# The experts' head: the first expert's rows picked from x by one-hot products on TensorE, and the second expert's rows turned inside the first gate product

## The chip, the cores and the metric

The kernel runs on one core of a Trainium2 chip. The metric is the device time of one launch in microseconds (us). An idle engine or a faster instruction counts only where the end of the launch moves. The five engines named here are TensorE (PE in the profile), VectorE (DVE), ScalarE (ACT), GpSimd (POOL) and SyncE (SP, which here only issues DMAs).

## What is computed

Two layers of a first kind are followed by two layers of a second kind, on 512 tokens of width 1024. The change touches only the mixture of experts at the end of each layer of the first kind, so it acts twice per launch:

```python
def _hier_moe(x, wg, bg, we, be, w_gate, w_up, w_down):
    ...
    ep, ei = lax.top_k(jax.nn.softmax(elog, -1), TOP_K)
    ep = ep / jnp.sum(ep, -1, keepdims=True)
    eid = gi * EXPERTS_PER_GROUP + ei
    combine = jnp.sum(jax.nn.one_hot(eid, N_EXPERTS, dtype=F32) * (gp * ep)[..., None], axis=2)
    h = jax.nn.silu(jnp.einsum('bsd,edf->bsef', x, w_gate)) * jnp.einsum('bsd,edf->bsef', x, w_up)
    h = h * combine[..., None].astype(h.dtype)
    return jnp.einsum('bsef,efd->bsd', h, w_down)
```

Each token uses 2 of 16 experts. The kernel gathers the up to 128 tokens of an expert into 128 slots, computes the expert for these rows alone, and scatters the results back.

## The kernel before

Every engine runs its own list of instructions in the order in which the code writes them; between engines only semaphores order the work. Nothing is planned by a scheduler, so an instruction written behind a waiting one waits too.

`expert_stage` (lines 2449 to 2740) treats 16 experts, e = 0 to 15, in a fixed order. The router ahead of it leaves `rank` (for each token and expert the slot number, or none) and `facts` (token number, row number, weight). For each expert, the steps are:

- **place(e)** (DVE, L2632) compares the slot numbers with the ranks. It gives `take`, a one-hot matrix of 4 tiles of 128 tokens by 128 slots. Two buffers alternate.
- **find_facts(e)** (PE, L2519): 4 products of `take` with the facts. **keep_facts(e)** (DVE, L2637 to L2639) turns them into `to_token`, `to_row` and `weight`, and signals `index_ready`. place(e+2) and, on PE, find_facts(e+1) wait for these.
- **gather(e)** (POOL, L2711), an indirect DMA, fetches the expert's rows of x from memory into `xg`, which has three buffers. `xg` is cleared first (L2722), because empty slots are not fetched.
- **turn_x(e)** (PE, L2530): 8 transposes of `xg` into two PSUM banks. **x_pair(e)** (ACT, L2588) copies each bank as the rounded part `xt_hi`, and **x_rest(e)** (DVE, L2645) computes the remainder `xt_lo`.
- **gate_up_product(e)** (PE, L240 to L242): 24 matmuls, 12 for each half of the 1024 rows of weights, into one bank.
- ACT applies silu (L2609), DVE multiplies (L2678, `hidden`), PE transposes the result (**turn_hidden**, L2550), ACT and DVE split it (L2615, L2686), and PE multiplies it with the down weights (12 matmuls). The result is scattered (L2718).

Weights arrive in units of 1 MB through a ring of six raw buffers (L2397). Each unit is split by ACT into its rounded part (`split_hi`, L2404) and by DVE, or POOL for the down weights, into the remainder (`split_lo`, L2408). SP loads unit u only when unit u-6 is split. The gate and up weights of expert 0 are units 0 and 1, those of expert 1 units 2 and 3.

The head is what stands ahead of the loop over the experts. On DVE: place(0), place(1), then keep_facts(e) and place(e+2) for e = 0 to 3, then split_lo of units 0 and 1, then x_rest(0) and x_rest(1). On PE: find_facts(0) to (3), turn_x(0), turn_x(1). On ACT: split_hi of units 0 and 1, x_pair(0), x_pair(1). In the loop's first round ACT splits units 2 and 3 and then applies silu, and DVE splits units 2 and 3 and then computes hidden(0). A whole second pass over the experts would run where an expert has more than 128 tokens; the profiled execution has one pass per layer.

Of the kernel before, what the change touches and what calls it, by code (L numbers as in the profile page):

```python
# [1773 lines left out]
def out_ffn_stage(env, stage, first, first_ffn, yt, xo, x, gains, small, out, saved):  # L1774
# [44 lines left out]
    with ExitStack() as local:  # L1819
# [133 lines left out]
        with nc.Block() as block:  # L1953
# [237 lines left out]
            def _(dve):  # L2191
# [148 lines left out]
                for m in range(len(downs)):  # L2340
# [13 lines left out]
                 "hidden_turned", "hidden_hi", "hidden_lo", "down_done", "stored_first", "stored_second", "rows_sent", "rows_seen")  # L2354
# [94 lines left out]
def expert_stage(env, gate_up, down, rank, facts, next_units, small, x, lower_rows, entry_loads):  # L2449
# [15 lines left out]
     hidden_lo, down_done, stored_first, stored_second, rows_sent, rows_seen) = (env.sem("experts", n) for n in EXPERT_EVENTS)  # L2465
# [9 lines left out]
    with ExitStack() as local:  # L2475
# [10 lines left out]
        og = tile("out", 2, D)  # L2486

# [3 lines left out]
        with nc.Block() as block:  # L2491
# [21 lines left out]
            def _(pe):  # L2513
# [8 lines left out]

                def turn_x(e):
                    pe.wait_ge(gathered[e % 3], 16 * (e // 3 + 1))
                    for b in range(2):
                        if e:
                            pe.wait_ge(x_lo, 2 * (e - 1) + b + 1)
                        for j in range(4):
                            k = 4 * b + j
                            last = nc.tensor.transpose(x_bank(b)[:, j, :], xg[:, e % 3, k * P:(k + 1) * P], ident)  # L2530
                        last.then_inc(x_turned, 1)

                def gate_up_product(e):
# [3 lines left out]
                    for half in range(2):  # L2537
# [5 lines left out]
                        last.then_inc(w.used, 1)  # L2543

# [25 lines left out]
                turn_x(0)  # L2570
                turn_x(1)
# [12 lines left out]
            def _(act):  # L2584
# [13 lines left out]
                for e in range(2):  # L2598
                    x_pair(e)
                for e in range(E):  # L2600
                    if e + 1 < E:
                        for half in range(2):
                            w.split_hi(act, w.at["gu", e + 1] + half)
                    if e == E - 1:
                        w.split_hi(act, w.at["down", e])
# [19 lines left out]
            def _(dve):  # L2625
# [32 lines left out]

                place(0)
# [6 lines left out]
                for e in range(2):  # L2666
                    x_rest(e)
                for e in range(E):
                    if e + 1 < E:
                        for half in range(2):  # L2670
                            w.split_lo(v, w.at["gu", e + 1] + half)
                    if e == E - 1:
                        w.split_lo(v, w.at["down", e])
# [32 lines left out]
            def _(pool):  # L2706
# [15 lines left out]
                nc.gpsimd.memset(xg[:, :, :], 0.0).then_inc(padded, 1)  # L2722
                pool.wait_ge(padded, 1)
                for e in range(3):
                    gather(e)
                for e in range(E):
# [8 lines left out]
                for s in range(3):  # L2735
                    pool.wait_ge(gathered[s], 16 * len(range(s, E, 3)))
# [842 lines left out]
```

## Time and profile before

| | us |
|---|---|
| median of 3 runs | 2600.57 |
| lowest and highest | 2599.93, 2602.46 |
| the profiled execution, whole | 2597.38 |
| its span, first to last instruction | 2595.6 |

PE is busy for 92% of the span, DVE 68%, ACT 51%, POOL 24%. The times in the rows below are counted from the span's start. A row of the timeline begins with the start and the duration of a group of equal instructions; "x8" is their count; the brackets at its end hold how long the engine stood idle ahead of the group and who ended that.
### The profile page before, as it was taken

To read this page: it belongs to the slowest core of one execution; us is meant where nothing else is said; L and a number is where in the kernel's file an instruction comes from. 1 tells how busy PE (TensorE), PEld (TensorE's weight loads), DVE (VectorE), ACT (ScalarE), POOL (GpSimd) and SP (SyncE) were. 2 spreads that over 40 slices of the span, in tenths; PEclk is the share of its full clock that TensorE was granted. 3 is DMA by queue.
4 is the path that set the end of the run, shared out by engine and by line. 5 is a ranking of instruction groups with operands and counts; after the bars stand their busy time and mean duration, and the time that the engine had idled before them with its cause. 6 is when DMAs were issued, how large, how long until landed. Compare 5 with 4: busy or idle time off the path is not lost. (4 is left out here: it accounts for less than half of the span.)

```text
span 2595.6 us, 37232 instructions
## 1 busy us (share of the span) xinstructions
PE 2391.2 (92%) x14216; PEld 2015.2 (78%) x14216; DVE 1752.6 (68%) x2747; ACT 1318.1 (51%) x2638; POOL 614.4 (24%) x337
## 2 busy tenths in 40 slices
PE   7999896997999896996998899999999989999999
PEld 7866675776866775775786789998887857899987
DVE  1755757874655756876698669995256985699942
ACT  3446625773546615775655744444157456444421
POOL 2401304771401303782360110000023501100000
PEclk9999987998999987998998999999999999999999
DMA  4210027983210017993120023323222201123221
GB/s 161 81 39 1 1 99 288 353 331 125 83 49 1 1 58 285 349 335 135 66 98 17 5 91 118 111 82 106 85 91 73 91 1 48 72 102 116 100 87 72
DMA packets 54994, 285.84 MB, mean 110 GB/s; under 512 B 13216, under 2 KB 13216, under 8 KB 28704
## 3 DMA queue, kind: packets, MB, share of 16 engines
q1 hardware_dynamic: 45600, 266.65, 28.1%
q0 software_dynamic: 9216, 16.80, 1.7%
q8 instruction: 114, 1.87, 0.3%
q14 instruction: 64, 0.52, 0.1%
HBM read 275.02 MB, written 25.17 MB: 116 GB/s over the span
## 5 line engine op out<-in xcount | busy, mean ns | idle before, releaser
L229 POOL TENSOR_TENSOR weights_lo<-weights_raw,weights_hi 128x2048 fp32r<-128x2048 f32 (+4 forms) x53 | 239.2, 4515 | 729.7 <-issue 358.6
L240 PE MATMUL ps<-x_operands,weights_hi 128*128 128x256 f32 x1232 | 347.7, 282 | 5.8 <-DVE weights_lo L1945 5.1
L241 PE MATMUL ps<-x_operands,weights_hi 128*128 128x256 f32 x1232 | 348.8, 283 | 0.0
L242 PE MATMUL ps<-x_operands,weights_lo 128*128 128x256 f32 x1232 | 348.2, 283 | 0.0
L215 ACT ACTIVATE weights_hi<-weights_raw 128x2048 fp32r<-128x2048 f32 (+5 forms) x86 | 148.2, 1723 | 307.9 <-PE ps L242 288.4
L240 PEld LDWEIGHTS ps<-x_operands,weights_hi 128*128 128x128 f32 x1232 | 233.7, 190 | 8.4 <-DVE weights_lo L1945 6.8
L242 PEld LDWEIGHTS ps<-x_operands,weights_lo 128*128 128x128 f32 x1232 | 231.7, 188 | 0.0
L241 PEld LDWEIGHTS ps<-x_operands,weights_hi 128*128 128x128 f32 x1232 | 231.0, 187 | 0.0
L240 PE MATMUL ps<-weights_hi,attn_ht_hi 128*128 128x512 f32 (+2 forms) x576 | 204.7, 355 | 4.3 <-DVE weights_lo L229 2.3
L241 PE MATMUL ps<-weights_lo,attn_ht_hi 128*128 128x512 f32 (+2 forms) x576 | 201.2, 349 | 0.0
L242 PE MATMUL ps<-weights_hi,attn_ht_lo 128*128 128x512 f32 (+2 forms) x576 | 200.5, 348 | 0.0
L229 DVE TENSOR_TENSOR weights_lo<-weights_raw,weights_hi 128x2048 fp32r<-128x2048 f32 (+3 forms) x33 | 65.1, 1973 | 179.6 <-ACT weights_hi L215 179.6
L240 PE MATMUL ps<-weights_hi,x_operands 128*128 128x512 f32 x384 | 152.9, 398 | 6.2 <-PEq L263 6.2
L241 PE MATMUL ps<-weights_lo,x_operands 128*128 128x512 f32 x384 | 152.9, 398 | 0.0
L240 PE MATMUL ps<-weights_hi,xt_hi 128*128 128x480 f32 (+2 forms) x384 | 138.9, 362 | 5.8 <-DVE weights_lo L229 2.5
L1939 ACT ACTIVATE weights_hi<-ffn_w_sums 128x1024 fp32r<-128x1024 f32 x66 | 70.0, 1060 | 133.4 <-DVE ffn_w_sums L2249 133.4
L242 PE MATMUL ps<-weights_hi,xt_lo 128*128 128x480 f32 (+2 forms) x384 | 136.1, 354 | 0.0
L241 PE MATMUL ps<-weights_lo,xt_hi 128*128 128x480 f32 (+2 forms) x384 | 135.8, 354 | 0.0
L240 PEld LDWEIGHTS ps<-weights_hi,attn_ht_hi 128*128 128x128 f32 x576 | 110.1, 191 | 28.0 <-issue 9.1
L242 PE MATMUL ps<-weights_hi,ffn_hidden_lo 128*128 128x512 f32 x320 | 125.8, 393 | 0.0
L242 PEld LDWEIGHTS ps<-weights_hi,attn_ht_lo 128*128 128x128 f32 x576 | 109.9, 191 | 13.4
L241 PEld LDWEIGHTS ps<-weights_lo,attn_ht_hi 128*128 128x128 f32 x576 | 110.2, 191 | 11.7
(531 smaller groups left out, 6259.5 us busy)
## 6 DMA issues: line engine op xcount, KB each, us to landing
weights_raw<-in_stream SPq DMA_DIRECT2D x96, 1024.0 KB, 4.7
weights_raw<-in_expert_gu SPq DMA_DIRECT2D x34, 1024.0 KB, 9.5
expert_raw<-in_expert_gu SPq DMA_DIRECT2D x30, 1024.0 KB, 9.7
expert_raw<-in_expert_down SPq DMA_DIRECT2D x18, 1024.0 KB, 8.5
weights_raw<-in_expert_down SPq DMA_DIRECT2D x14, 1024.0 KB, 8.2
weights_raw<-in_stream SPq DMA_DIRECT2D x12, 960.0 KB, 4.5
ffn_raw<-in_stream SPq DMA_DIRECT2D x10, 1024.0 KB, 4.8
weights_raw<-in_stream SPq DMA_DIRECT2D x8, 700.0 KB, 9.5
```

The costliest lines, as they stand in the source:

```text
L215: self.nc.scalar.activation(self.split_tiles(u)[0][:, 0:n], self.env.raw[:, u % self.RAW, 0:n], ACT.Copy).then_inc(self.hi_ready, 1)
L229: eng.tensor_tensor(lo[:, 0:n], self.env.raw[:, u % self.RAW, 0:n], hi[:, 0:n].bitcast(F32), ALU.subtract).then_inc(self.lo_ready, 1)
L240: nc.tensor.matmul(out, a[0], b[0], start=start, stop=False, **more)
L241: nc.tensor.matmul(out, a[0], b[1], start=False, stop=False, **more)
L242: return nc.tensor.matmul(out, a[1], b[0], start=False, stop=stop, **more)
L1939: nc.scalar.activation(ring(g)[0], quarter(c, w_of[p]), ACT.Copy).then_inc(w_hi_done, 1)
```

## The change

Expert 0's rows are no longer gathered. DVE writes its one-hot matrix a second time, in float32, into the space of `hidden` (`first_take`), ahead of place(0). PE multiplies x, which lies in SBUF, with it (`pick_x`): for each of 8 chunks of 128 columns 4 products, one for each tile of tokens. This gives the transposed rows directly in the bank where turn_x(0) put them. The picks are written between the find_facts of the head, two chunks behind each. turn_x(1) moves from the head into the middle of gate_up_product(0); x_pair(1) on ACT and x_rest(1) on DVE move between the splits of units 2 and 3. POOL clears each buffer of `xg` by itself and gathers experts 1 and 2 in between; gather(3) no longer waits behind a gather(0).

```diff
@@ expert_stage
+        first_take = hidden[:, :, :].rearrange("p a c -> p (a c)").rearrange("p (t s) -> p t s", t=T)
...
+                def pick_x(chunks):
+                    pe.wait_ge(first_placed, 1)
+                    for k in chunks:
+                        for t in range(T):
+                            last = nc.tensor.matmul(x_bank(k // 4)[:, k % 4, :], x[:, t, k * P:(k + 1) * P],
+                                                    first_take[:, t, :], start=(t == 0), stop=(t == T - 1))
+                    if k % 4 == 3:
+                        last.then_inc(x_turned, 1)
+
...
                         last.then_inc(w.used, 1)
+                        if e == 0 and half == 0:
+                            turn_x(1)
...
                 for e in range(AHEAD):
                     find_facts(e)
-                turn_x(0)
-                turn_x(1)
+                    pick_x(range(2 * e, 2 * e + 2))
...
                 for half in range(2):
                     w.split_hi(act, half)
-                for e in range(2):
-                    x_pair(e)
+                x_pair(0)
...
                             w.split_hi(act, w.at["gu", e + 1] + half)
+                            if e == 0 and half == 0:
+                                x_pair(1)
...
+                v.tensor_tensor(first_take, env.slot_numbers.unsqueeze(1).to_broadcast([P, T, SLOTS]),
+                                per_tile(rank[:, :, EXPERT_ORDER[0]], SLOTS), ALU.is_equal).then_inc(first_placed, 1)
                 place(0)
                 place(1)
...
-                for e in range(2):
-                    x_rest(e)
+                x_rest(0)
...
                             w.split_lo(v, w.at["gu", e + 1] + half)
+                            if e == 0 and half == 0:
+                                x_rest(1)
...
-                nc.gpsimd.memset(xg[:, :, :], 0.0).then_inc(padded, 1)
-                pool.wait_ge(padded, 1)
-                for e in range(3):
+                for e in (1, 2):
+                    nc.gpsimd.memset(xg[:, e, :], 0.0).then_inc(padded, 1)
+                    pool.wait_ge(padded, e)
                     gather(e)
+                nc.gpsimd.memset(xg[:, 0, :], 0.0).then_inc(padded, 1)
+                pool.wait_ge(padded, 3)
```

PE's list at the head of the expert stage, before (L2519 are the facts, L2530 the turned rows of experts 0 and 1, `weights_hi` the first gate product):

```order
L2519 MATMUL ps<-slot_facts,expert_take 128x4 x16
L2530 MATMUL ps<-consts,expert_xg 128x128 x16
L240 MATMUL ps<-weights_hi,expert_xt_hi 128x512
L241 MATMUL ps<-weights_lo,expert_xt_hi 128x512
L242 MATMUL ps<-weights_hi,expert_xt_lo 128x512
```

The same place after (L2521 are the facts, L2529 the picks):

```order
L2521 MATMUL ps<-slot_facts,expert_take 128x4 x4
L2529 MATMUL ps<-expert_hidden,x 128x128 x8
L2521 MATMUL ps<-slot_facts,expert_take 128x4 x4
L2529 MATMUL ps<-expert_hidden,x 128x128 x8
L2521 MATMUL ps<-slot_facts,expert_take 128x4 x4
L2529 MATMUL ps<-expert_hidden,x 128x128 x8
L2521 MATMUL ps<-slot_facts,expert_take 128x4 x4
L2529 MATMUL ps<-expert_hidden,x 128x128 x8
```

The facts of experts 1, 2 and 3 now stand behind 8, 16 and 24 picks, and the 8 transposes of expert 1 behind the first 12 matmuls of the gate product.

ACT's list there, before (L2404 is split_hi, L2588 x_pair, L2609 silu):

```order
L2404 ACTIVATE weights_hi<-weights_raw 128x2048 x2
L2588 ACTIVATE expert_xt_hi<-ps 128x512 x4
L2404 ACTIVATE expert_w_hi<-weights_raw 128x2048
L2404 ACTIVATE expert_w_hi<-expert_raw 128x2048
L2609 ACT_TABLE_LOAD
L2609 ACTIVATE expert_gate<-ps 128x256
```

And after (L2405 is split_hi, L2600 x_pair, L2622 silu):

```order
L2405 ACTIVATE weights_hi<-weights_raw 128x2048 x2
L2600 ACTIVATE expert_xt_hi<-ps 128x512 x2
L2405 ACTIVATE expert_w_hi<-weights_raw 128x2048
L2600 ACTIVATE expert_xt_hi<-ps 128x512 x2
L2405 ACTIVATE expert_w_hi<-expert_raw 128x2048
L2622 ACT_TABLE_LOAD
L2622 ACTIVATE expert_gate<-ps 128x256
```

The split of unit 3 now stands behind the copies of expert 1's turned rows; on DVE the remainders move in the same way.

## Rows read from the trace of the kernel before

**Rows 1.** Timeline of PE, layer 1's head: start, us, line, count, [idle before].
```profile
401.50 1.01 PE L2519 MATMUL ps<-slot_facts,expert_take 128*128 128x4 f32 x4 [4.70 <-DVE expert_take L2632]
...
413.52 1.97 PE L2530 MATMUL ps<-consts,expert_xg 128*128 128x128 f32 x8 [6.63 <-DMA expert_xg<-x_rows,expert_token]
417.29 1.97 PE L2530 MATMUL ps<-consts,expert_xg 128*128 128x128 f32 x8 [1.80 <-DMA expert_xg<-x_rows,expert_token]
418.91 0.78 PE L240 MATMUL ps<-weights_hi,expert_xt_hi 128*128 128x512 f32 x1
...
420.34 0.63 PE L240 MATMUL ps<-weights_hi,expert_xt_hi 128*128 128x512 f32 x1
420.77 0.50 PE L241 MATMUL ps<-weights_lo,expert_xt_hi 128*128 128x512 f32 x1
...
421.33 0.40 PE L240 MATMUL ps<-weights_hi,expert_xt_hi 128*128 128x512 f32 x1
...
424.15 0.39 PE L240 MATMUL ps<-weights_hi,expert_xt_hi 128*128 128x512 f32 x1
```
**Rows 2.** Window in the loop: us, busy PE, PEld, DVE, ACT, POOL, PEclk, DMA, GB/s.
```profile
442.00:462.00 20.00, 19.39 (x98) 15.81 (x97) 17.06 (x23) 15.13 (x16) 14.95 (x7) 1.00 0.94 348
```
**Rows 3.** Timeline of PE, the hidden transposes of experts 0 and 1.
```profile
426.70 0.44 PE L2550 MATMUL ps<-consts,expert_hidden 128*128 128x128 f32 x2 [0.99 <-DVE expert_hidden L2678]
...
438.06 0.44 PE L2550 MATMUL ps<-consts,expert_hidden 128*128 128x128 f32 x2 [1.28 <-DVE expert_hidden L2678]
```
**Rows 4.** Timeline of DVE, layer 1's head and first two rounds.
```profile
400.75 1.29 DVE L2632 TENSOR_TENSOR expert_take<-consts,expert_rank 128x512 fp32r<-128x512 f32 x2 [2.78 <-PEq L120]
...
406.93 0.16 DVE L2637 TENSOR_SCALAR expert_token<-ps 128x1 int32<-128x1 f32 x1 [0.57 <-PE ps L2519]
...
407.13 0.68 DVE L2632 TENSOR_TENSOR expert_take<-consts,expert_rank 128x512 fp32r<-128x512 f32 x1
...
423.94 2.28 DVE L2408 TENSOR_TENSOR expert_w_lo<-expert_raw,expert_w_hi 128x2048 fp32r<-128x2048 f32 x1
426.17 0.48 DVE L2678 SCALAR_TENSOR_TENSOR expert_hidden<-expert_gate,expert_weight,ps 128x256 f32<-128x256 f32 x1
428.24 0.42 DVE L2686 TENSOR_TENSOR expert_ht_lo<-ps,expert_ht_hi 128x256 fp32r<-128x256 f32 x1 [1.59 <-ACT expert_ht_hi L2615]
...
430.13 3.08 DVE L2632 TENSOR_TENSOR expert_take<-consts,expert_rank 128x512 fp32r<-128x512 f32 x1
...
437.54 0.47 DVE L2678 SCALAR_TENSOR_TENSOR expert_hidden<-expert_gate,expert_weight,ps 128x256 f32<-128x256 f32 x1
```
**Rows 5.** Groups of PE by line and shape: count, busy, mean ns, idle before.
```profile
L3280 PE MATMUL ps<-proj,attn_prob_t 128*128 128x128 f32 x160 | 26.7, 305 | 0.0
```
**Rows 6.** Timeline of PE elsewhere: float32 work at the half and the full clock.
```profile
237.06 3.46 PE L1200 MATMUL ps<-consts,cols 128*128 128x128 f32 x16 [3.07 <-PEq L1331]
...
1402.67 1.49 PE L3280 MATMUL ps<-proj,attn_prob_t 128*128 128x128 f32 x6
1404.09 0.92 PE L3251 MATMUL ps<-qk_t 64*128 64x384 f32 x4
...
1439.87 1.06 PE L3280 MATMUL ps<-proj,attn_prob_t 128*128 128x128 f32 x8
```
**Rows 7.** Windows over stretches in which the clock rose or didn't, columns as in rows 2.
```profile
400.00:417.00 17.00, 5.94 (x24) 5.28 (x24) 10.82 (x22) 6.30 (x5) 7.14 (x5) 0.50 0.91 362
...
240.30:243.70 3.40, 3.40 (x10) 1.58 (x10) 1.83 (x3) 3.40 (x11) 0.91 (x2) 1.00 0.00 0
1398.50:1404.00 5.50, 5.50 (x23) 4.49 (x23) 5.12 (x15) 3.21 (x13) 0.00 (x0) 0.50 0.00 1
```
**Rows 8.** Timeline of ACT, layer 1's first round.
```profile
421.59 1.91 ACT L2404 ACTIVATE expert_w_hi<-expert_raw 128x2048 fp32r<-128x2048 f32 x1
423.52 1.28 ACT L2609 ACT_TABLE_LOAD   x1
```
**Rows 9.** Timeline of POOL, layer 1's head.
```profile
400.71 2.66 POOL L2722 MEMSET expert_xg<- 128x3072 f32 x1 [84.41 <-issue]
```

More of the change, by code:

```diff
@@ L2353 @@
 EXPERT_EVENTS = ("padded", "placed", "facts_ready", "index_ready", "x_turned", "x_hi", "x_lo", "silu_done", "hidden_done",
-                 "hidden_turned", "hidden_hi", "hidden_lo", "down_done", "stored_first", "stored_second", "rows_sent", "rows_seen")
+                 "hidden_turned", "hidden_hi", "hidden_lo", "down_done", "stored_first", "stored_second", "rows_sent", "rows_seen",
+                 "first_placed")
 class ExpertWeights:
@@ L2464, in expert_stage @@
     (padded, placed, facts_ready, index_ready, x_turned, x_hi, x_lo, silu_done, hidden_done, hidden_turned, hidden_hi,
-     hidden_lo, down_done, stored_first, stored_second, rows_sent, rows_seen) = (env.sem("experts", n) for n in EXPERT_EVENTS)
+     hidden_lo, down_done, stored_first, stored_second, rows_sent, rows_seen, first_placed) = (env.sem("experts", n) for n in EXPERT_EVENTS)
     gathered = [env.sem("experts", f"gathered{s}") for s in range(3)]
@@ L2521, in find_facts @@
                     last.then_inc(facts_ready, 1)
+                def pick_x(chunks):
[6 more added lines that the diff above has]
+                        last.then_inc(x_turned, 1)
                 def turn_x(e):
-                    pe.wait_ge(gathered[e % 3], 16 * (e // 3 + 1))
+                    pe.wait_ge(gathered[e % 3], 16 * len(range(e % 3 or 3, e + 1, 3)))
                     for b in range(2):
@@ L2735, in _ @@
                 for s in range(3):
-                    pool.wait_ge(gathered[s], 16 * len(range(s, E, 3)))
+                    pool.wait_ge(gathered[s], 16 * len(range(s or 3, E, 3)))
                 for s in range(2):
```

## The prediction, made before the changed kernel ran

> **What bounds the kernel now.** I read the timeline of each engine over the head of layer 1's expert stage first, then the windows for TensorE's clock. Layer 2 runs the same code with the same counts, so what layer 1 gives counts twice. The stage begins at 400.7, and PE then stands idle: 6.63 us until expert 0's gathered rows land at 413.5, and 1.80 us more for expert 1's [rows 1]. The first gate product starts at S = 418.91, behind the transposes of expert 1. In the loop behind the head PE is busy 19.39 of 20 us [rows 2], so what the head loses or gains at the start of that dense part stays. Between the two lies one more place to look at: turn_hidden(0) at 426.70 and turn_hidden(1) at 438.06 both wait for DVE, 0.99 and 1.28 us [rows 3]. From the second of them on PE runs without a wait of size. So 438.06 is the point at which I settle the account: how much later or earlier does turn_hidden(1) come?
>
> Three engines must deliver for S: PE the turned rows, ACT the rounded copies, and DVE the remainders. DVE was free early: its last facts began at 406.93, the last place at 407.13, the two weight splits followed, and then it waited for the turned rows [rows 1, 4].
>
> **Removed: the waits for two gathers.** They are worth 6.63 and 1.80 us on PE [rows 1], if nothing else takes their place. The rest of this part asks what does.
>
> **Added: the picks, and what they hold up.** first_take is one more compare on DVE: two of them take 1.29 us together, 0.68 alone [rows 4], so each costs 0.6. find_facts(0) moves from 401.50 [rows 1] to 402.1. A pick is a float32 product. In the trace each such product of the code is two instructions: L3280 of this shape, 80 products in the code's list over both layers, stands there 160 times [rows 5]. So 32 picks are 64 instructions. Six of L3280 at the half clock take 1404.09 - 1402.67 = 1.42 us, 0.237 each; eight at the full clock take about 0.12 each [rows 6]. The clock is 0.50 over the whole head [rows 7]. Sixteen transposes of the same size, begun at the half clock, take 3.46, about 0.21 each [rows 6]; that is the lower bound, and I take 0.235. The 4 fact products of an expert cost 0.96 at the half clock [rows 1]. For DVE what counts is when the facts of expert 3 are out: behind 4 groups of facts and 3 groups of 16 pick instructions. At the half clock that is 4 x 0.96 + 48 x 0.235 = 15.1 us.
>
> The picks keep PE busy, so the clock should rise under them. Before, the steps of the matmuls fall from 0.43 (420.34 to 420.77) to 0.235 (12 from 421.33 to 424.15), so it rose at about 421.1, 3.8 us after the unbroken work that began at 417.29 [rows 1]. It rose within 3.2 us after the transposes that began at 237.06; yet it stayed at the half for the 5.5 us of unbroken work from 1398.5 [rows 1, 6, 7]. I take 4.8 us, so 406.9, with 3.1 and 5.6 as ends. The other 10.3 us of half-clock work then take 0.51 of that, and the facts of expert 3 are out at 406.9 + 5.3 = 412.2, where before it was 406.9.
>
> The Trainium skill (TensorE: Matmul & The Clock Gate, Part 1) says that the point at which the clock rises is run-variable for the same kernel. These rows differ likewise, 3.1 us to over 5.5. By one fixed ramp of 3.8 us, facts would be out at 411.7, and the sum would be lower by about 1 us a layer.
>
> DVE cannot go on without these facts, because keep_facts(3) and place(5) stand ahead of its weight splits. From the end of the facts it needs 0.04 to begin, 0.20 to the place, 0.6 for it, 2 x 2.23 for two splits back to back, the distance from one's start to the next instruction at 423.94, and 1.29 for the two halves of x_rest(0), the same size as two places [rows 4]: together 6.6. So x_lo is complete at 418.75, and with 0.05 for the signal S = 418.8. ACT is no hindrance: the picks end at 412.2 + 16 x 0.12 = 414.1, and its two copies are done before DVE wants them at 417.5. **The gather's wait is thus replaced by a wait for DVE, and the gain of S is 0.1 us.** With the ends of the ramp, S is 417.9 to 419.2.
>
> **Moved: turn_x(1) into the gate product.** Before, its 8 transposes lay ahead of S. Now PE does 12 matmuls, 8 transposes, 12 matmuls. What follows hangs on T, the time at which the transposes are done: x_pair(1), then split_hi of unit 3 on ACT, split_lo of unit 3 on DVE, and only then hidden(0). From T, ACT's split of unit 3 begins 0.55 later and takes 1.9 [rows 8]; DVE's split follows at once and hidden(0) starts 2.23 after the split's start, as 423.94 to 426.17 [rows 4]. With the signals that is T + 4.73, and turn_hidden(0) is 0.53 later [rows 3, 4], T + 5.26. The silu path is shorter: the second 12 matmuls end at T + 2.8 and ACT's table load of 1.28 at T + 3.7 [rows 8].
>
> From hidden(0) to hidden(1) it was 11.37 us, of which DVE waited 1.59 for ACT [rows 4], which now has less of a backlog when hidden(0) comes; I count 0.6 of it as regained. hidden(1) comes at T + 4.73 + 10.77 = T + 15.5, and turn_hidden(1) at T + 16.0. PE's own path, two products and a down product, would be ready for it at T + 15.2.
>
> **T itself.** At the full clock T = S + 12 x 0.235 + 8 x 0.11 + 0.15 = S + 3.85 [rows 1]. But PE stands idle from 414.1 to 418.8, 4.7 us. In this trace the idle 3 us ahead of 237.06 were enough for 0.50 [rows 6, 7]. So the product starts at the half clock, as before; only that before, the 8 transposes had already used up 1.6 us of the ramp. The half-clock price of 12 matmuls and 8 transposes is 12 x 0.43 + 8 x 0.22 + 0.15 = 7.07; with a ramp of 4.8 again, T = S + 4.8 + 2.27 x 0.53 + 0.15 = S + 6.15 = 424.95.
>
> turn_hidden(1) = 440.95, against 438.06 [rows 3]: **2.9 us later in layer 1**, and as much in layer 2. Sum: +5.8 us. The rest of the stage shifts along: SP loads units 6 and 7 about 5 us later, since their buffers are split later, but the loop asks for them only at its third expert. gather(1) is written behind facts that come at 408, and PE asks for it at 424, in the middle of the product; before, it landed at 417.2 even behind a gather(0) [rows 1]. gather(2) and gather(3) have more room still.
>
> **A port rule.** POOL now clears `xg` in three pieces, and two of them lie beside DVE's later places. Before, the clearing from 400.71 to 403.37 lay over two places at 0.6 each, as fast as alone [rows 4, 9]; the place at 430.13, beside a POOL tensor operation, took 3.08. I cost the clearing at nothing. The Trainium skill (GPSIMD Engine Reference, 1. Specifications) has GpSimd's SBUF interfaces shared with VectorE, with contention for instructions of two SBUF inputs. These rows agree for the tensor operation and not for the clearing.
>
> **The rivals.**
> 1. The clock is already full, or rises at once, under the picks: facts of expert 3 at 402.1 + 7.7 = 409.8, S = 416.4, then the product at full clock, T = 420.3, turn_hidden(1) at 436.3: -1.8 a layer, -3.6 in all, 2597.0. It decides from T under 422. For it: the picks are unbroken work. Against: 0.50 for the 17 us from 400 [rows 7]. A chance of 0.04; over 0.2% faster would need still more, such as DVE getting its facts without waiting for picks.
> 2. The clock holds through PE's idle 4.7 us: T = S + 3.85, turn_hidden(1) at 438.65, +0.6 a layer: 2601.8. Chance 0.16.
> 3. The downstream chain takes up more than 0.6 us, or the ramp is short both times: +1 to +2 a layer, 2603 to 2604.5. Chance 0.2.
> 4. The clearing or the gathers' issue slow DVE's place(4) and place(5), one of them to 3.08 as beside the tensor operation: +2.4 a layer more than the forecast, 2611.2. Chance 0.06.
> 5. The picks do not raise the clock: facts at 417.2, S = 423.8, T = S + 6.15: +8 a layer, 2616. Against: 16 such transposes from 237.06 raised it by 240.3 [rows 6, 7]. Chance 0.05.
>
> **How the numbers follow.** The forecast, with 0.49, is +5.8 us: profiled 2597.4 + 5.8 = 2603.2, and since that execution lay 3.2 us under the median, 2600.6 + 5.8 = 2606.4. Its own range, from the two ends of each ramp, is +4 to +8. The range of 8 in 10 takes in rival 3, most of 2 and rival 4: 2601.5 to 2611.5. Within 0.2%, 5.2 us, is about what a measurement of this kernel can tell from no change. Slower by more: two thirds of the forecast (0.33), rivals 4 and 5, some tails (0.06): 0.50. Faster: 0.03. Same: 0.47.
>
> **What would show it.** In the changed profile: 64 pick instructions, the first at about 403; the clock rising between 405 and 408; PE's last facts near 412; DVE's two splits from 413 to 417.5; S near 418.8, waiting for DVE's remainder and not for a DMA; the half clock over most of the first 12 matmuls; turn_hidden(1) near 441. The prediction is wrong if DVE begins its splits before 411, if the clock is 1.00 at S, or if turn_hidden(2) follows turn_hidden(1) by less than the 10.35 us of PE's round, which would mean slack that I do not see.

## The result and the profile after

The changed kernel takes **2608.67 us** (median of 12 runs, 2602.49 to 2611.92); the kernel before, in 12 runs beside it, 2600.25 (2597.91 to 2603.96). The ratio is 1.0031, with a 95% interval of 1.0024 to 1.0039: slower by 8.4 us, 0.3%. The forecast was 2606.4, range 2601.5 to 2611.5. Of the runs reported below, one of experiment 5 (3996 us) and two of the kernel before (3990 and 6726 us) are left out of the ratios; without them no median below moves by more than 0.3 us.

| profiled execution | before | after |
|---|---|---|
| whole time, us | 2597.38 | 2609.35 |
| span, us | 2595.6 | 2607.6 |
| PE busy, us | 2391.2 | 2412.0 |
| mean granted clock | 0.959 | 0.957 |

The profiled pair differs by 12.0 us where the medians differ by 8.4. Of the 12.0, the two heads hold 7.9; 0.4 lie ahead of the first head, 1.8 between the heads and 1.9 behind the second, in steps of about 1 us, in stages in which the two kernels are the same. At one such step the clock differs: it is 0.50 in 740.5 to 743.5 us after, and 1.00 in the same place before, 734.2 to 737.2.

The account of a head runs as the prediction set it up, from its first DVE instruction to turn_hidden(1):

| from the head's first DVE instruction, us | before, layer 1 | after, layer 1 | before, layer 2 | after, layer 2 |
|---|---|---|---|---|
| first gate product (S) | 18.16 | 18.44 | 17.76 | 18.40 |
| turn_hidden(0) | 25.95 | 29.14 | 25.76 | 29.09 |
| turn_hidden(1) | 37.31 | 42.47 | 37.14 | 39.92 |
| against before | | +5.16 | | +2.78 |

So the gathers' wait is gone, and S is still 0.3 and 0.6 us later than before. From turn_hidden(1) of layer 1 the distance stays: turn_hidden(2) follows 10.37 us later before and 10.35 after.

First PE's timeline in layer 1, the answer to [rows 1] and [rows 3] (start, us, engine, line, operation, count, [idle before]). L2521 are the facts, L2529 the picks, L240 the gate product, L2541 the turned rows, L2563 the hidden transposes.

```profile
402.47 1.02 PE L2521 MATMUL ps<-slot_facts,expert_take 128*128 128x4 f32 x4 [5.30 <-DVE expert_take L2645]
403.35 3.76 PE L2529 MATMUL ps<-expert_hidden,x 128*128 128x128 f32 x16
406.76 0.99 PE L2521 MATMUL ps<-slot_facts,expert_take 128*128 128x4 f32 x4
...
410.61 2.03 PE L2529 MATMUL ps<-expert_hidden,x 128*128 128x128 f32 x16
412.40 0.59 PE L2521 MATMUL ps<-slot_facts,expert_take 128*128 128x4 f32 x4
412.84 2.03 PE L2529 MATMUL ps<-expert_hidden,x 128*128 128x128 f32 x16
...
419.56 0.79 PE L240 MATMUL ps<-weights_hi,expert_xt_hi 128*128 128x512 f32 x1 [4.69 <-DVE expert_xt_lo L2658]
...
423.96 1.04 PE L2541 MATMUL ps<-consts,expert_xg 128*128 128x128 f32 x8
...
430.26 0.69 PE L2563 MATMUL ps<-consts,expert_hidden 128*128 128x128 f32 x2 [2.46 <-DVE expert_hidden L2694]
430.74 1.91 PE L2541 MATMUL ps<-consts,expert_xg 128*128 128x128 f32 x8
...
443.59 0.41 PE L2563 MATMUL ps<-consts,expert_hidden 128*128 128x128 f32 x2 [0.30 <-PE ps L242]
```

The 6.63 us for a DMA ahead of the turned rows [rows 1] are now 4.69 for DVE's remainder, ahead of S. The wait ahead of turn_hidden(0) has grown from 0.99 to 2.46, and the wait of 1.28 ahead of turn_hidden(1) [rows 3] is gone, because PE itself is late there. In layer 2 the same two places read:

```profile
1024.21 0.44 PE L2563 MATMUL ps<-consts,expert_hidden 128*128 128x128 f32 x2 [2.45 <-DVE expert_hidden L2694]
...
1035.04 0.44 PE L2563 MATMUL ps<-consts,expert_hidden 128*128 128x128 f32 x2 [0.76 <-DVE expert_hidden L2694]
```

The picks, in the view of one line (the shortest, median and longest duration of one in ns; 64 instructions in each layer):

```profile
L2529 PE MATMUL ps<-expert_hidden,x x128: 274/275/561, 403.3 to 1008.6; 128*128 128x128 f32 x128
```

Spacing is what counts, not this latency: group to group, 16 picks took 406.76 - 403.35 = 3.41 us at the half clock, 0.213 each, and 412.40 - 410.61 = 1.79 at the full clock, 0.112 each.

DVE's timeline, the answer to [rows 4]:

```profile
413.02 0.16 DVE L2650 TENSOR_SCALAR expert_token<-ps 128x1 int32<-128x1 f32 x1 [1.34 <-PE ps L2521]
...
413.23 0.68 DVE L2645 TENSOR_TENSOR expert_take<-consts,expert_rank 128x512 fp32r<-128x512 f32 x1
413.82 4.49 DVE L2409 TENSOR_TENSOR weights_lo<-weights_raw,weights_hi 128x2048 fp32r<-128x2048 f32 x2
...
418.23 1.28 DVE L2658 TENSOR_TENSOR expert_xt_lo<-ps,expert_xt_hi 128x512 fp32r<-128x512 f32 x2
...
425.22 1.29 DVE L2658 TENSOR_TENSOR expert_xt_lo<-ps,expert_xt_hi 128x512 fp32r<-128x512 f32 x2 [3.51 <-ACT expert_xt_hi L2600]
...
427.52 2.29 DVE L2409 TENSOR_TENSOR expert_w_lo<-expert_raw,expert_w_hi 128x2048 fp32r<-128x2048 f32 x1 [1.01 <-ACT expert_w_hi L2405]
...
429.73 0.47 DVE L2694 SCALAR_TENSOR_TENSOR expert_hidden<-expert_gate,expert_weight,ps 128x256 f32<-128x256 f32 x1
```

The two splits stand behind facts that PE delivers only between its picks; behind the splits stands x_rest(0), which S needs. Below it, the chain that the move of turn_x(1) made: copies, split on ACT, split on DVE, hidden(0).

The windows for the clock, the answer to [rows 7] and [rows 2] (us; busy PE, PEld, DVE, ACT, POOL with counts; then PE's granted clock, DMA share, GB/s). The last is layer 2.

```profile
402.50:409.20 6.70, 6.70 (x31) 6.70 (x32) 2.30 (x9) 2.18 (x2) 0.16 (x1) 0.50 0.97 401
408.60:414.50 5.90, 5.90 (x53) 5.90 (x52) 2.45 (x10) 2.40 (x2) 4.15 (x4) 0.95 1.01 425
419.60:422.50 2.90, 2.90 (x7) 2.32 (x8) 2.11 (x1) 0.00 (x0) 0.00 (x0) 0.50 0.97 357
423.00:427.50 4.50, 4.50 (x25) 3.65 (x23) 1.29 (x2) 2.89 (x3) 0.00 (x0) 1.00 0.96 395
430.30:436.00 5.70, 5.70 (x21) 5.12 (x22) 3.80 (x7) 4.06 (x5) 4.79 (x2) 0.50 0.54 187
442.00:462.00 20.00, 19.39 (x98) 15.77 (x97) 16.96 (x23) 14.94 (x17) 15.53 (x6) 1.00 0.84 300
1024.30:1031.00 6.70, 6.70 (x37) 5.78 (x38) 5.68 (x8) 5.63 (x6) 5.84 (x2) 1.00 0.57 175
```

The fifth row is the difference between the layers. Behind the idle 2.46 us PE worked at the half clock for about 6 us in layer 1 (430.30 to 436.00), and in layer 2, behind an idle 2.45, it did not (1024.30 to 1031.00). The slow stretch of PE also holds up ACT and, through it, DVE's chain to hidden(1):

```profile
437.83 1.92 ACT L2405 ACTIVATE expert_w_hi<-weights_raw 128x2048 fp32r<-128x2048 f32 x1 [2.75 <-PE ps L242]
...
439.78 2.29 DVE L2409 TENSOR_TENSOR expert_w_lo<-weights_raw,expert_w_hi 128x2048 fp32r<-128x2048 f32 x1 [1.40 <-ACT expert_w_hi L2405]
```

POOL's timeline, the answer to [rows 9]:

```profile
409.04 1.21 POOL L2727 DMA_INDIRECT expert_xg<-x_rows,expert_token  x1 [7.00 <-DVE expert_weight L2652]
410.26 0.97 POOL L2739 MEMSET expert_xg<- 128x1024 f32 x1
...
413.03 0.97 POOL L2742 MEMSET expert_xg<- 128x1024 f32 x1
```

The clearing from 413.03 lies over DVE's place from 413.23, which took 0.68, as long as alone.

### The profile page after: what moved, and what is told of

Same layout as the page of the kernel before. It is cut to its first block and busy times, and to the rows that moved or that the text cites. A ratio compares the mean times of both kernels' runs of the same rounds, so it can differ in the third digit from the quotient of the medians.

```text
span 2607.6 us, 37460 instructions
## 1 busy us (share of the span) xinstructions
PE 2412.0 (93%) x14328; PEld 2030.2 (78%) x14328; DVE 1751.2 (67%) x2749; ACT 1320.0 (51%) x2638; POOL 611.5 (23%) x339
## 5 line engine op out<-in xcount | busy, mean ns | idle before, releaser
L240 PE MATMUL ps<-x_operands,weights_hi 128*128 128x256 f32 x1232 | 349.3, 284 | 5.7 <-DVE weights_lo L1945 5.1
L240 PEld LDWEIGHTS ps<-x_operands,weights_hi 128*128 128x128 f32 x1232 | 231.3, 188 | 8.4 <-DVE weights_lo L1945 6.8
L240 PE MATMUL ps<-weights_hi,attn_ht_hi 128*128 128x512 f32 (+2 forms) x576 | 203.8, 354 | 5.0 <-DVE weights_lo L229 2.3
L240 PE MATMUL ps<-weights_hi,x_operands 128*128 128x512 f32 x384 | 152.9, 398 | 6.7 <-PEq L263 6.6
L240 PE MATMUL ps<-weights_hi,xt_hi 128*128 128x480 f32 (+2 forms) x384 | 138.1, 360 | 6.1 <-DVE weights_lo L229 2.5
L240 PEld LDWEIGHTS ps<-weights_hi,attn_ht_hi 128*128 128x128 f32 x576 | 109.4, 190 | 28.9 <-issue 9.1
L242 PEld LDWEIGHTS ps<-weights_hi,attn_ht_lo 128*128 128x128 f32 x576 | 109.6, 190 | 13.3
```

The costliest lines, as they stand in the source:

```text
L240: nc.tensor.matmul(out, a[0], b[0], start=start, stop=False, **more)
L242: return nc.tensor.matmul(out, a[1], b[0], start=False, stop=stop, **more)
```

## Experiments

All are edits of the changed kernel and compute the whole output; each was timed in 11 runs, beside runs of the kernel before on the same chip: 33 for experiments 1 to 4, 33 for 5 to 8, 27 for 9 to 11. "After" is the changed kernel. A ratio is that to the kernel before, with its 95% interval; times given as differences are of medians. The last two columns of the table at the end of this section compare each head sum with the time.

**1. DVE's splits ahead of the last facts.** The theory: S waits for DVE, and DVE for facts behind picks.

```diff
                 for e in range(AHEAD):
+                    if e >= 2:
+                        w.split_lo(v, e - 2)
                     keep_facts(e)
                     place(e + 2)
-                for half in range(2):
-                    w.split_lo(v, half)
                 x_rest(0)
```

> The changed kernel with one edit on DVE: the split of unit 0 stands ahead of keep_facts(2) and that of unit 1 ahead of keep_facts(3), instead of both behind keep_facts(3). Theory (DVE, held up by facts that stand behind the picks, sets the start S of the first gate product): S comes about 2.9 us sooner in each layer (416.6 on the scale of the changed profile, where it was 419.56), PE's idle gap ahead of S shrinks from 4.7 to under 2 us, the launch is 6 to 9 us faster than the changed kernel, about 2600 to 2602. Rival (the first product would then wait for something else, or the loss lies in the moved transposes alone): under 2 us gained against the changed kernel, 2607 or more.

Measured: 2599.69 against 2599.28, ratio 1.0002 (0.9993 to 1.0011). S comes 14.90 and 14.81 us behind the head's start, 3.5 sooner than after, and the launch is 8 to 9 us faster than after, as the theory had it. PE's timeline, layer 1:

```profile
416.04 0.50 PE L240 MATMUL ps<-weights_hi,expert_xt_hi 128*128 128x512 f32 x1 [1.79 <-DVE expert_xt_lo L2658]
...
419.93 1.09 PE L2541 MATMUL ps<-consts,expert_xg 128*128 128x128 f32 x8 [0.81 <-DMA expert_xg<-x_rows,expert_token]
...
426.28 0.44 PE L2563 MATMUL ps<-consts,expert_hidden 128*128 128x128 f32 x2 [2.45 <-DVE expert_hidden L2694]
```

DVE's, with the splits now in the stretches in which it waited for facts:

```profile
408.01 0.68 DVE L2645 TENSOR_TENSOR expert_take<-consts,expert_rank 128x512 fp32r<-128x512 f32 x1
408.69 2.29 DVE L2409 TENSOR_TENSOR weights_lo<-weights_raw,weights_hi 128x2048 fp32r<-128x2048 f32 x1
411.10 0.68 DVE L2645 TENSOR_TENSOR expert_take<-consts,expert_rank 128x512 fp32r<-128x512 f32 x1
411.70 2.29 DVE L2409 TENSOR_TENSOR weights_lo<-weights_raw,weights_hi 128x2048 fp32r<-128x2048 f32 x1
414.10 0.68 DVE L2645 TENSOR_TENSOR expert_take<-consts,expert_rank 128x512 fp32r<-128x512 f32 x1
```

Mending DVE's order alone takes back the whole loss of the change. It pays twice: S is sooner, and the gap ahead of it is 1.79 instead of 4.69, and the product starts at the full clock (the first matmul takes 0.50 us, where it took 0.79 in the changed kernel). The 2.45 ahead of turn_hidden(0) is still there. A new wait of 0.81 for gather(1) stands ahead of the transposes. On POOL the issue of that gather now takes 3.02 us instead of 1.21, beside DVE's first split:

```profile
409.05 3.02 POOL L2727 DMA_INDIRECT expert_xg<-x_rows,expert_token  x1 [7.00 <-DVE expert_weight L2652]
```

**2. turn_x(1), with its copies and remainders, back ahead of the gate product.** The theory: the move made hidden(0) late. PE's part of the edit; x_pair(1) on ACT and x_rest(1) on DVE go back behind x_pair(0) and x_rest(0) likewise.

```diff
                         last.then_inc(w.used, 1)
-                        if e == 0 and half == 0:
-                            turn_x(1)
...
                     pick_x(range(2 * e, 2 * e + 2))
+                turn_x(1)
```

> The changed kernel with the second half of the change undone: expert 1's rows are turned ahead of the first gate product again, and copied and split right behind those of expert 0. Theory (turning them inside the product delays hidden(0), since unit 3 is split behind them): S comes later, 420 to 421, since PE waits for gather(1), but hidden(0) comes about 2 us sooner (427.8 instead of 429.73), the launch is 3 to 5 us faster than the changed kernel, 2603 to 2606. Rival (the wait for gather(1) only takes the place of the delay): within 1.5 us of the changed kernel.

Measured: 2602.79, 1.0010 (1.0001 to 1.0019). S is 0.4 and 0.8 later than after, hidden(0) 2.5 and 1.8 sooner, turn_hidden(1) 37.67 and 38.62 behind the head's start. So the moved step costs more inside the product than it would ahead of it. One stated reason, that PE would wait for gather(1), fell:

```profile
418.27 1.94 PE L2541 MATMUL ps<-consts,expert_xg 128*128 128x128 f32 x8 [4.18 <-DVE expert_xt_lo L2656]
```

The transposes waited for DVE's x_rest(0), which clears the bank that they write, and not for gather(1), which was issued at 408.95 and had landed 8.6 us later, at about 417.6; DVE's first half of x_rest(0) ended at 418.1.

**3. PE kept busy up to S.** 40 transposes of x into an unused bank behind the picks; nothing reads them.

```diff
                     pick_x(range(2 * e, 2 * e + 2))
+                for _ in range(40):
+                    nc.tensor.transpose(ps[:, BT, 0:P], x[:, 0, 0:P], ident)
```

> The changed kernel with 40 further transposes of x into a PSUM bank that nobody reads at that time, behind the picks, to fill 4.4 us of PE's 4.7 us of idle time ahead of S. Theory (the idle gap halves the clock for the first 3 us of the gate product): S unchanged, clock 1.00 at S, T 1.2 us sooner in each layer, 2.4 us gained in all, more where the second half-clock stretch of layer 1 vanishes too: 2603 to 2606.5. Rival (the clock falls for another reason, or what it gives back is hidden behind ACT and DVE): no gain against the changed kernel.

Measured: 2604.45, 1.0023 (1.0014 to 1.0032). That is 0.0008 or 2 us under after by the ratios and 3.2 by the medians, and the two intervals overlap. S is where it was (18.10, 18.45), the first matmul takes 0.50, and turn_x(1) starts 2.91 behind S instead of 4.40. That is the price of the half-clock start alone, 1.5 us a layer. turn_hidden(1) comes at 39.39 and 39.64, since the gap of 2.45 ahead of turn_hidden(0) stayed, and behind it the clock fell in both layers. The window behind turn_hidden(0), layer 1:

```profile
426.60:429.60 3.00, 3.00 (x13) 2.71 (x12) 2.47 (x7) 2.65 (x4) 3.00 (x1) 0.50 0.77 322
```

**4. The splits of unit 3 ahead of expert 1's copies and remainders,** on ACT and on DVE, with turn_x(1) where the change put it.

```diff
                         for half in range(2):
                             w.split_hi(act, w.at["gu", e + 1] + half)
-                            if e == 0 and half == 0:
-                                x_pair(1)
+                        if e == 0:
+                            x_pair(1)
...
                             w.split_lo(v, w.at["gu", e + 1] + half)
-                            if e == 0 and half == 0:
-                                x_rest(1)
+                        if e == 0:
+                            x_rest(1)
```

> The changed kernel with unit 3 split by ACT and DVE ahead of the copies of expert 1's turned rows (x_pair(1) and x_rest(1) behind both splits of the first round). Theory (hidden(0) hangs on T + split + split): unit 3 is split while PE is in the first half of the product, hidden(0) follows the product's end by 0.6 us, turn_hidden(0) comes 1.6 us sooner, PE's idle gap ahead of it falls from 2.46 to 1 us and the clock stays full behind it in layer 1: 3 to 6 us gained in all, 2603 to 2605.5. Rival (hidden(1) is bound by the splits of units 5 and 6 anyway): the gap moves to turn_hidden(1), under 1.5 us gained.

Measured: 2602.88, 1.0011 (1.0002 to 1.0020). S as after (18.16, 18.38), hidden(0) 1.9 and 1.5 sooner, turn_hidden(1) 38.62 and 38.95. DVE and PE, layer 1:

```profile
427.50 0.48 DVE L2694 SCALAR_TENSOR_TENSOR expert_hidden<-expert_gate,expert_weight,ps 128x256 f32<-128x256 f32 x1 [1.75 <-ACT expert_gate L2622]
...
428.04 0.44 PE L2563 MATMUL ps<-consts,expert_hidden 128*128 128x128 f32 x2 [0.99 <-DVE expert_hidden L2694]
```

hidden(0) now waits for the silu, which can't come before the product's end, and the gap is back at the 0.99 of the kernel before [rows 3].

**5. The facts earlier on PE:** one chunk of picks behind each find_facts and four behind them all.

```diff
                     find_facts(e)
-                    pick_x(range(2 * e, 2 * e + 2))
+                    pick_x([e])
+                pick_x(range(AHEAD, KD))
```

> The changed kernel with one edit on PE alone: one chunk (8 instructions) of picks behind each expert's facts instead of two, and the other four chunks behind all facts. DVE's list is as in the changed kernel. Theory (the facts of expert 3 are late because 48 pick instructions stand ahead of them): with 24 ahead, DVE's last facts begin at 409.8 instead of 413.0, S comes at 416.5 instead of 419.56, and the launch is 5 to 8 us faster than the changed kernel: 2600 to 2603. Rival (S was held by DVE's weight splits for another reason, such as their data landing late): S within 1 us of the changed kernel, 2606 or more.

Measured: 2602.77 against 2600.18, 1.0010 (1.0000 to 1.0019). S at 15.05 and 16.81, and turn_hidden(1) at 35.09 and 36.84, sooner than before the change. The theory's S held in layer 1 and not in layer 2, where the clock rose only 10.2 us behind PE's first instruction instead of 5.2:

```profile
991.20:1001.30 10.10, 10.10 (x47) 10.10 (x48) 4.58 (x18) 3.82 (x2) 4.03 (x4) 0.50 0.98 408
```

The two profiled heads give 2.5 us less than before, but the median is 2.6 more. These heads each had the gap of 2.44 and no fall of the clock. A fall in other executions would add about 2.5 us to a head, and a late rise as in layer 2 adds 1.75; that these make up the difference is not shown, because the profiled execution itself took 2602.28, close to the median, with no fall in either head. Against the profiled execution of before its excess lies outside the heads, 7.4 us. So the cause of the difference stays open.

**6. Both orders together (1 and 4).**

> The first and the fourth experiment together: DVE splits units 0 and 1 ahead of the facts of experts 2 and 3, and unit 3 is split ahead of expert 1's copies. Theory (the two delays stand one behind the other in time, S and then hidden(0)): both gains add up, turn_hidden(1) comes 34.5 us after the start of the head, where the kernel before needs 37.2 and the first experiment 36 to 38: 3 to 5 us faster than the kernel before, 2594 to 2596.5. Rival (the wait for gather(1) in the middle of the product, 0.8 us in the first experiment, or DVE's chain from hidden(0) to hidden(1) takes one of them back): within 1.5 us of the kernel before.

Measured: 2596.69 against 2600.18, 0.9985 (0.9976 to 0.9994), a hair above the expected range and under both kernels. PE, layer 1:

```profile
413.97 0.50 PE L240 MATMUL ps<-weights_hi,expert_xt_hi 128*128 128x512 f32 x1 [1.41 <-DVE expert_xt_lo L2658]
...
418.20 1.09 PE L2541 MATMUL ps<-consts,expert_xg 128*128 128x128 f32 x8 [1.17 <-DMA expert_xg<-x_rows,expert_token]
...
423.09 0.44 PE L2563 MATMUL ps<-consts,expert_hidden 128*128 128x128 f32 x2 [0.99 <-DVE expert_hidden L2694]
```

Here the removed wait is a gain in the end. Whether such an order of DVE's list would also help the kernel before, where DVE was free early, no run tests. The wait for expert 1's gather shows up again, 1.17 us, in the middle of the product, and turn_hidden(1) waits 1.29 for hidden(1), as before the change [rows 3].

**7. All three orders:** the facts early, both weight splits ahead of keep_facts(3), the splits of unit 3 first.

```diff
                 for e in range(AHEAD):
+                    if e == AHEAD - 1:
+                        for half in range(2):
+                            w.split_lo(v, half)
                     keep_facts(e)
...
-                for half in range(2):
-                    w.split_lo(v, half)
```

The other edits of this kernel are those of 5 and 4.

> One chunk of picks behind each expert's facts, both weight splits ahead of keep_facts(3), and unit 3 split ahead of expert 1's copies. Theory: S at 416.1 on the scale of the changed profile, now bound by the end of the picks; gather(1) is issued 2 us sooner and PE doesn't wait for it; turn_hidden(1) comes 34 us after the start of the head: 4 to 6.5 us faster than the kernel before, 2593.5 to 2596. Rival (the floor is reached in the sixth kernel already): equal to it within 1 us.

Measured: 2596.59, 0.9986 (0.9977 to 0.9995), the same as 6, as the rival had it. S comes at 16.58 and 16.83, later than the 14.89 and 15.18 of 6: here the clock rose only 9.8 and 10.2 us behind PE's first instruction (6.2 and 6.6 in 6), so the picks ended late. ACT's second copy of expert 0's rows waits 2.98 for them in both layers, and the second half of x_rest(0) waits 1.13 and 1.87 for that copy.

**8. The facts early, and turn_x(1) ahead of the product (2 and 5).** It was to tell whether the lateness of gather(1) is what makes the early place of turn_x(1) dear.

> The fifth kernel, with expert 1's rows turned ahead of the first gate product again, as before the change: picks alone, with early facts. Theory (with DVE free early, the wait for gather(1) decides S): gather(1) is issued at 406.5 to 407.5 and lands at 416 to 417, S is 418 to 419 as in the kernel before, and the launch is within 2 us of the kernel before. Rival (the moved transposes cost in any case, so that undoing them always gains): 3 us or more faster than the fifth kernel.

Measured: 2599.40, 0.9999 (0.9990 to 1.0008), 3.4 us under 5. That is within the 2 us of before that the theory wanted, and it also meets the rival's mark, 3 us under 5; so this run does not part them by its time. The layers differ. In layer 1 no half of turn_x(1) waits for a DMA, and the second waits for DVE:

```profile
414.68 0.60 PE L2541 MATMUL ps<-consts,expert_xg 128*128 128x128 f32 x4
...
416.26 0.65 PE L2541 MATMUL ps<-consts,expert_xg 128*128 128x128 f32 x4 [0.98 <-DVE expert_xt_lo L2657]
```

In layer 2 it waits for gather(1), as the theory wanted, and behind this wait the clock fell:

```profile
1001.43 1.09 PE L2541 MATMUL ps<-consts,expert_xg 128*128 128x128 f32 x8 [2.37 <-DMA expert_xg<-x_rows,expert_token]
```

What parts them is the clock under the picks (windows of layer 1 and of layer 2):

```profile
399.50:412.30 12.80, 12.75 (x59) 12.75 (x60) 7.28 (x19) 4.42 (x3) 4.16 (x4) 0.50 0.97 402
987.40:992.60 5.20, 5.20 (x25) 5.20 (x25) 2.32 (x9) 1.71 (x1) 0.42 (x1) 0.50 0.91 383
```

Where PE stayed at the half clock for 12.8 us, the gather had landed when PE asked for it; where it stayed for 5.2, it had not.

By the medians, 2 against after and 8 against 5 say the same thing in two settings: the move of turn_x(1) into the product, with the split of unit 3 behind its copies, costs 3 to 5 us. In the second setting the profiled heads don't bear it out: those of 8 are 2.1 us later than those of 5.

**9 to 11. The changed kernel again, 6 again and 4 again,** on one chip.

> The changed kernel unedited, on the chip of the next two runs. Theory: a gap of about 2.45 us of PE ahead of turn_hidden(0) stands in both layers' heads, and behind it the clock falls in some heads and not in others (so far in 4 of 8 heads with this gap, in the profiles of the changed kernel and of three edits). So the head costs +2.8 us without the fall and +5.2 with it, two layers: +5.6 to +10.4, a median of 2606 to 2610, and single times spread wider than the kernel before's. Rival: the first measurement was a matter of that chip; then the median is under 2605, the same as with both splits first.

> The kernel with DVE's weight splits ahead of the last facts and the splits of unit 3 ahead of expert 1's turned rows, again. Theory: gap ahead of turn_hidden(0) 0.99 in both heads, clock 1.00 behind it in both; 10 to 13 us under the changed kernel on this chip, 2 to 5 us under the kernel before (2596 to 2598 by a before of 2600). Rival, that its gain was an accident of one measurement: within 1.5 us of the kernel before.

> Only the splits of unit 3 ahead of expert 1's turned rows, beside the changed kernel on the same chip. Theory: it takes away the 2.45 us gap (0.99 is left) and with it every second fall of the clock; hidden(0) comes 1.5 to 1.9 us sooner, turn_hidden(1) 1 us sooner where the clock did not fall and 3.5 to 4 where it did. With a fall in half the heads that is 4 to 5 us under the changed kernel. Rival, that the fall costs nothing by the end of the stage: 2 us under it.

Measured, with the kernel before at 2600.63: after took 2607.43 (2602.75 to 2612.76), 1.0029 (1.0020 to 1.0038); 6 again 2597.11, 0.9989 (0.9980 to 0.9998), 10.3 under after; 4 again 2603.33, 1.0014 (1.0005 to 1.0023), 4.1 under after. In this profile of after the layers have changed places. Windows behind turn_hidden(0), layer 1 and layer 2:

```profile
427.80:433.00 5.20, 5.20 (x28) 4.38 (x27) 5.07 (x8) 4.39 (x5) 5.04 (x2) 1.00 0.44 183
1021.50:1027.00 5.50, 5.50 (x20) 4.78 (x19) 4.53 (x8) 3.13 (x4) 5.35 (x2) 0.52 0.46 176
```

turn_hidden(1) stands 39.52 and 42.43 behind the head's start, where the first profile had 42.47 and 39.92. Against 4 again (38.48, 38.94) a head without the fall lies 1.0 later and one with it 3.5.

All the heads together. "Head sum" is turn_hidden(1) from the head's start, both layers, less the 74.45 of before; "time" is the difference of the medians on the same chip.

| kernel | gap ahead of turn_hidden(0), layers 1, 2 | clock fell behind it | head sum, us | time, us |
|---|---|---|---|---|
| before | 0.99, 0.99 | no, no | 0 | 0 |
| after | 2.46, 2.45 | yes, no | +7.9 | +8.4 |
| after again | 2.45, 2.44 | no, yes | +7.5 | +6.8 |
| 1 | 2.45, 2.46 | no, yes | -0.5 | +0.4 |
| 2 | 1.25, 0.99 | no, no | +1.8 | +3.5 |
| 3 | 2.45, 2.45 | yes, yes | +4.6 | +5.2 |
| 4 | 0.99, 0.99 | no, no | +3.1 | +3.6 |
| 4 again | 0.99, 0.99 | no, no | +3.0 | +2.7 |
| 5 | 2.44, 2.44 | no, no | -2.5 | +2.6 |
| 6 | 0.99, 0.99 | no, no | -4.5 | -3.5 |
| 6 again | 0.99, 0.99 | no, no | -5.0 | -3.5 |
| 7 | 0.99, 0.99 | no, no | -2.8 | -3.6 |
| 8 | 1.79, 0.99 | yes, no | -0.4 | -0.8 |

But for 5, what a profile shows in the two heads stands within 2 us of what the medians show. The whole time of one profiled execution is a poorer witness: outside the heads, where all kernels are the same, these executions took 0 to 8 us more than the profiled one of before, 8.1 in 7, whose profiled execution took 2602.72 with a median of 2596.59.

## Why the prediction was right, and where not

**What bounds, and the replaced wait: right.** The forecast had S at 418.8, waiting for DVE's remainder, behind an idle 4.7. It came at 419.56 behind an idle 4.69, 0.37 of the distance being there at the head's start already. Experiment 1 shows the cause: without the facts ahead of the splits S is 3.5 us sooner.

**The cost of the picks: right in sum, by luck, as two errors nearly cancel.** A pick at the half clock takes 0.213, the lower bound, and not the 0.235 taken, and a group of facts 403.35 - 402.47 = 0.88 and not 0.96; the half-clock work ahead of the last facts is thus 4 x 0.88 + 48 x 0.213 = 13.7 us instead of 15.1. The clock rose at about 409.2, 6.7 us after PE began at 402.47, and not after the 4.8 taken, past the end of 5.6 that the range held and past the 408 that was named as a sign. DVE got the facts of expert 3 at 413.02 where 412.2 was forecast. The step of first_take was right: from the head's start to find_facts(0) 402.47 - 401.12 = 1.35, before 0.75.

**The half clock at S: right in kind, a little too dear.** The product started at 0.50, as forecast against rival 2, but the clock was back after about 3.3 us instead of 4.8: the 8 transposes were done at S + 5.4 where S + 6.15 was forecast. Experiment 3 prices this start at 1.5 us a layer.

**From T to hidden(0): right.** T is about 425.0, hidden(0) 429.73, turn_hidden(0) 430.26: T + 4.73 and T + 5.26, as worked out. Experiments 2 and 4 show it from both sides, by moving turn_x(1) back and by moving the split ahead of its copies. In layer 2, turn_hidden(1) follows 10.83 us later (forecast 10.74), and the head is 2.8 us dearer (forecast 2.9). That this sum fits so well is again luck: S came 0.6 us later than before where 0.1 sooner was forecast, and T followed S 0.7 us sooner than forecast.

**What was missed: the second fall of the clock.** The step that failed is "turn_hidden(1) = 440.95 ... and as much in layer 2". It took hidden(1)'s chain from hidden(0) to be DVE's alone and had PE ready in time, at T + 15.2. That holds only where the clock stays full. The forecast itself made turn_hidden(0) wait for 2.4 us (T + 2.8 to T + 5.26), but asked for the clock only at the gap ahead of S. In one layer of each profile of after the clock fell there, PE's round became 13.3 us instead of 10.8, and PE took DVE's place as the last to be ready. DVE's own chain stretched too, from 10.85 us between hidden(0) and hidden(1) to 12.26, as its split waited for ACT and ACT for PE. Such a head costs 5.2 and 5.3 us in the two profiles, one without the fall 2.8 and 2.2: in sum 7.9 and 7.5, for medians of 8.4 and 6.8 more than before, where 5.8 was forecast. So one fall is worth 2.4 to 3.1 us, as much as the median lies above the forecast in the first measurement (2.3 us); in the second the miss is 1.0.

**The rivals.** Rival 1 (full clock under the picks) and rival 5 (no rise) fell by the windows; rival 2 (the clock holds through 4.7 us) by the first matmul of 0.79 us; rival 4 by the place of 0.68 beside the clearing. None of the three signs that were to prove the forecast wrong came: DVE began its splits at 413.82, the clock at S was 0.50, and turn_hidden(2) follows turn_hidden(1) by 10.35. Of the signs that were to bear it out, two failed: the clock's rise between 405 and 408, and turn_hidden(1) near 441 in layer 1, where it came at 443.59. Rival 3 was right in one part (the ramp at S was short), worth 0.7 us.

## What to carry to other kernels

Where a wait for a transfer is removed by more work on an engine, look at what the other engines have queued behind that work's results: here two weight splits that needed none of it stood behind facts that did, and their order decided between 8 us lost and, with the other order mended too, 3.5 won. Price each new idle stretch of TensorE twice, once for itself and once for a fall of the clock behind it, also the short one that stands at the end of a chain. Where heads of the same code differ between the layers of one profile, count many heads before a cause is named, compare the stretch that was changed rather than the whole profiled execution, and time in many runs.

## What the runs showed that was not expected

**The clock's fall behind short gaps.** Of the gaps ahead of turn_hidden(0), the ten of 2.44 to 2.46 us had a fall behind them five times; the one of 1.79 had it; the fifteen of 0.99 to 1.25 never. Ahead of S, eight gaps of 4.69 us (after and 4, two profiles each) always gave a start at the half clock, and ten of 1.41 to 2.23 us (1, 5, 7 and both profiles of 6) never did. Ahead of turn_x(1), the two gaps of 4.18 and 4.19 us in 2 and the one of 2.37 in 8 had it as well. So near 2.4 us both outcomes occur. The same code has it in layer 1 in one run and in layer 2 in another. What sets it, no run here shows. Nor is it shown that a kernel with such gaps spreads more: the runs of after lie over 9.4 and 10.0 us in the two measurements, but those of 1, with the same gaps, over 5.1, and those of 6 and 7, without them, over 8.7, 6.7 and 9.0.

**The rise.** From PE's start at the head the clock came up after 5.3 to 6.8 us in all 18 heads with two chunks of picks behind each find_facts. In the six heads with one chunk (5, 7 and 8) it took 5.2 us twice and 9.8 to 12.8 four times, though PE was busy 12.75 of 12.80 us in the longest. Behind S it came up after 3.0 to 3.3 us in the changed kernel and in 4. The Trainium skill (TensorE: Matmul & The Clock Gate, Part 1) says that the point at which the clock rises varies between runs of the same kernel; these heads agree, and the two heads of one execution differ as well, by 4.9 us in 5 and 7.6 in 8.

**The gather's issue.** An issue of a gather on POOL that begins early under a weight split of DVE lasts 2.5 to 3.0 us and ends 0.9 to 1.1 us behind the end of that split, in nine places (1, 6, 7 and 6 again); elsewhere it mostly takes 1.0 to 1.3. In 1 and 6 that delays gather(1) by about 1.8 us, and PE then waits for it in the middle of the product in both layers of 1 and in layer 1 of 6.

**The port.** POOL's clearing of 128 x 1024 did not slow the place on DVE beside it (0.68 beside it and alone), while the place beside POOL's tensor operation from 431.06, which lasted 4.56 us, took 2.05, as one of 3.08 in [rows 4].
